# A hybrid decoder step: opening projections on unscaled rows, and the last expert outputs summed onto the residual in PSUM

## The reference, cut to what matters

```python
h = x * rsqrt(mean(x*x) + EPS) * norm1_g            # per row scale, per column gain
z = h @ w_in                                        # u (S5), xr, gate (RG-LRU), q, k, v, o, i/f gates (mLSTM)
# u goes through a diagonal complex SSM whose step sizes and angles come from
# exp(log_step), lambda_re, lambda_im; xr through a convolution and RG-LRU; q,k,v through chunked mLSTM
x1 = x + concat(s5, rglru, mlstm) @ w_out
g2 = rmsnorm(x1) * norm2_g
top4 = top_k(g2 @ router, 4); gates = softmax(top4)
for e in range(32):                                 # each token takes part in 4 experts
    y += gate[e] * (swiglu(g2 @ w1[e] + b1[e]) @ w2[e] + b2[e])
out = rmsnorm(x1 + y) * final_norm_g
```

## Time and profile before

| | us |
|---|---|
| time, median of 3 runs | 1101.66 (1099.63 to 1101.93) |
| the profiled execution, its own time | 1100.9 |
| its span | 1099.1 |
| TensorE busy | 1033.2 (94%) |
| VectorE, ScalarE, GpSimd busy | 317.2, 198.4, 95.4 |
| moved by DMA | 429.45 MB, mean 391 GB/s |

### The profile page before, as it was taken

The page is one execution under the profiler, slowest core; times in us unless marked ns, Lnnn a source line. Parts: engine busy times, 40 slices in busy tenths (PEclk is TensorE's granted clock), DMA queues, the critical chain, the costliest instruction groups (busy, mean ns, idle before and its releaser), DMA issues.

```text
span 1099.1 us, 13174 instructions
## 1 busy us (share of the span) xinstructions
PE 1033.2 (94%) x5132; PEld 434.6 (40%) x5132; DVE 317.2 (29%) x643; ACT 198.4 (18%) x418; POOL 95.4 (9%) x177
## 2 busy tenths in 40 slices
PE   8999999999999998999899988999899989998986
PEld 5767745334333433343333323332334233433322
DVE  6889456312131212120212112121212121202123
ACT  6543525301110201011000201020102010100002
POOL 6899000000000000000000000000000000000000
PEclk9999999999999999999999999999999999999999
DMA  7533799999999999999999999999999999999995
...
DMA packets 62052, 429.45 MB, mean 391 GB/s; under 512 B 12022, under 2 KB 25054, under 8 KB 33342
## 3 DMA queue, kind: packets, MB, share of 16 engines
...
## 4 chain that ended last, share of the span: by engine, by line
PE 53%; DMA 38%; DVE 5%; ACT 2%; issue 1%; SPq 1%; ACTq 0%; DVEq 0%
DMA ring_a<-in_exp_w_dram 32%; PE psum L2369 17%; PE psum L2404 12%; PE psum L2390 6%; DMA ring_b<-in_exp_w_dram 6%; PE psum L2303 3%; PE psum L2326 3%; PE psum L2134 3%; PE psum L1862 2%; PE psum L2413 1%; PE psum L2253 1%; PE psum L2259 1%; DVE rgb L1336 1%; SPq L444 1%; PE psum L2419 0%
## 5 line engine op out<-in xcount | busy, mean ns | idle before, releaser
L2369 PE MATMUL psum<-ring_a,xg 128*64 128x512 f32 x1200 | 341.8, 600 | 14.8 <-DMA ring_a<-in_exp_w_dram 14.8
L2404 PE MATMUL psum<-ring_a,aT 128*64 128x512 f32 x768 | 217.7, 596 | 9.9 <-DMA ring_a<-in_exp_w_dram 9.6
L2369 PEld LDWEIGHTS psum<-ring_a,xg 128*64 128x64 f32 x1200 | 102.8, 137 | 170.8 <-issue 165.4
L2369 PE MATMUL psum<-ring_b,xg 128*64 128x512 f32 x368 | 152.3, 598 | 7.7 <-DMA ring_a<-in_exp_w_dram 7.7
L1667 DVE TENSOR_TENSOR x<-x,psum 128x512 f32<-128x512 f32 x64 | 44.0, 687 | 384.1 <-PE psum L2326 384.1
L2390 PE MATMUL psum<-ring_a,xg 128*64 128x512 f32 x336 | 103.5, 609 | 14.5 <-DMA ring_b<-in_exp_w_dram 14.5
L2404 PEld LDWEIGHTS psum<-ring_a,aT 128*64 128x64 f32 x768 | 68.2, 137 | 111.8 <-issue 106.5
L2404 PE MATMUL psum<-ring_b,aT 128*64 128x512 f32 x256 | 104.1, 595 | 4.0 <-DMA ring_a<-in_exp_w_dram 2.5
L1736 DVE TENSOR_SCALAR acts<-psum 128x512 f32<-128x512 f32 x32 | 22.0, 687 | 224.4 <-PE psum L2390 208.0
L1040 ACT ACTIVATE acts<-acts 128x512 f32<-128x512 f32 x32 | 20.1, 627 | 297.5 <-DVE acts L1736 297.5
L2369 PEld LDWEIGHTS psum<-ring_b,xg 128*64 128x64 f32 x368 | 43.1, 136 | 75.5 <-issue 63.6
...
## 6 DMA issues: line engine op xcount, KB each, us to landing
...
```

The costliest lines, as they stand in the source:

```text
L2369: m = M(psum[64 * x:64 * x + 64, bk, :], xg[:, k, u, 64 * x:64 * x + 64], w[x][:, 512 * bk:512 * bk + 512], start=False, stop=(k == KD - 1))
L2404: m = M(psum[64 * x:64 * x + 64, 4 + nn, :], aT[:, 2 * j + s, 64 * x:64 * x + 64], w[x][:, 1024 * s + 512 * nn:1024 * s + 512 * nn + 512], ...
```

## The change

Five edits belong to the opening. The rows are turned as they arrive, without their scale: `turn_half` waits for the load alone, and all six halves go through VectorE, times `norm1_g`, into `raw_hT`, which lies where `q` and `k` come later. `u0` and `u1` are computed from `raw_hT`. The row scales become a row: TensorE spreads the three columns of `nst` over all partitions by products with the identity (bank `rstd`), in the middle of `u0`; ScalarE copies that to `rstd_row`; VectorE multiplies `raw_hT` by it into `hT` in two halves (`scaled`) and multiplies `u0` and `u1` by it on their way out of PSUM (`u_scaled`). The parameter rows are split: the 24 that are needed first (`norm1_g` and the lambdas) are in bank `vec`, the rest in `vec2`, turned within `u0`. ScalarE's exponential of the log steps comes first of all, one root is taken for all three tiles, and 14 warming products of TensorE become 9. SyncE issues the left half of the first weights before five of the parameter rows, and five loads of old states move from SyncE's queue to ScalarE's; TensorE turns those states after `xr0`, not before the gate products.

At the end, TensorE opens six result banks with a product whose columns are all zero while it waits for the last weights, VectorE copies the residual into them (`end_residuals`), and the six last combine products are added on top (`combine_end`). ScalarE and VectorE then read the sums in PSUM (`summed`), and the adding of VectorE goes.

```diff
-for _name, _n in (("norm1_g", 8), ("s5_d", 2), ("s5_glu_b", 2), ("rg_conv_w", 8), ("rg_conv_b", 2), ("rg_ba", 2),
-                  ("rg_bx", 2), ("rg_lambda", 2), ("ml_norm_g", 4), ("s5_lambda_re", 8), ("s5_lambda_im", 8)):
+for _name, _n in (("norm1_g", 8), ("s5_lambda_re", 8), ("s5_lambda_im", 8), ("s5_d", 2), ("s5_glu_b", 2), ("rg_conv_w", 8),
...
+NFIRST = 24
...
+_place(["vec", "vec2"], (6,))
+_place(["rstd"], (7,))
...
+        raw_hT = qkT[:].rearrange("p (k t) -> p k t", k=KD)
+        rstd_row = uT_rolled[:, 1, :]
...
+        def summed(i):
+
+            b = (6, 0, 2)[i]
+            return psum[0:TILES[i][1], b:b + 2, :].rearrange("p b n -> p (b n)")
...
-        END_UNITS = [(0, 0), (0, 1), (1, 0), (1, 1), (2, None)]
-        ADDED = (2, 4, 8)
+        END_UNITS = [(0, 0), (0, 1), (1, 0), (1, 1), (2, 0), (2, 1)]
+        END_BANKS = (6, 7, 0, 1, 2, 3)
...
+            for name, src in LAMBDAS:
+                load_vector(sp, name, src)
+            sp.dma_start(slot_view(0, 512)[:, :, 0:256], w_in_cols(WCH[0][0], 256)).then_inc(sem("w_in0"), 16)
...
-            A(nst[:, 12:13], nst[:, 8:9], ACT.Sqrt).then_inc(says_now("table_loaded"), 1)
+            act.wait_ge(sem("step_loaded"), 16)
+            A(step2[:], step2[:], ACT.Exp).then_inc(sem("step_exp"), 1)
             for i, (t0, n) in enumerate(TILES):
                 act.wait_ge(sem(f"x_loaded{i}"), 16)
                 A(x1[0:n, i, :], xn[0:n, i, :], ACT.Square, accum_out=nst[0:n, i:i + 1]).then_inc(says_now("ms_ready"), 1)
-                act.wait_ge(*at("ms_ready", i + 1))
-                A(nst[:, 4 + i:5 + i], nst[:, i:i + 1], ACT.Sqrt, scale=1.0 / D, bias=nst[:, 8:9]).then_inc(says_now("root_ready"), 1)
-            await_fill(act, "vec")
-            A(vecs[:, 0:NVEC + J5], bank("vec")[:, 0:NVEC + J5], ACT.Copy).then_inc(drained[FILLS["vec"][0]], 1)
-            act.wait_ge(drained[FILLS["vec"][0]], 1)
-            for i in range(2):
-                name = f"hT{2 * i + 1}"
-                await_fill(act, name)
-                for c in range(4):
-                    m = A(hT[:, 4 + c, 128 * i:128 * i + 128], bank(name)[:, 128 * c:128 * c + 128], ACT.Copy, scale=vec("norm1_g", 4 + c))
-                m.then_inc(drained[FILLS[name][0]], 1)
+            act.wait_ge(*at("ms_ready", 3))
+            A(nst[:, 4:7], nst[:, 0:3], ACT.Sqrt, scale=1.0 / D, bias=nst[:, 8:9]).then_inc(says_now("root_ready"), 1)
...
+            await_fill(act, "vec2")
+            A(vecs[:, NFIRST:NVEC], bank("vec2")[:, NFIRST:NVEC], ACT.Copy).then_inc(drained[FILLS["vec2"][0]], 1)
+            act.wait_ge(drained[FILLS["vec2"][0]], 2)
...
+            copy_out("rstd", rstd_row, bank("rstd")[:, 0:T])
...
-                await_fill(act, f"u{x}")
+                act.wait_ge(sem("u_scaled"), x + 1)
                 for half_ in range(2):
-                    A(uT_rolled[64 * half_:64 * half_ + 64, x, :], bank(f"u{x}")[64 - 64 * half_:128 - 64 * half_, 0:T], ACT.Copy).then_inc(
+                    A(uT_rolled[64 * half_:64 * half_ + 64, x, :], uT[64 - 64 * half_:128 - 64 * half_, x, :], ACT.Copy).then_inc(
                         sem("u_rolled"), 1)
-                act.wait_ge(sem("u_rolled"), 2 * x + 2)
-                copy_out(f"u{x}", uT[:, x, :], bank(f"u{x}")[:, 0:T])
 
             u_out(0)
+            u_out(1)
...
-                    A(psum[0:rows_, 4:6, :].rearrange("p b n -> p (b n)"), x1[0:rows_, i, :], ACT.Square,
+                    A(psum[0:rows_, 4:6, :].rearrange("p b n -> p (b n)"), summed(i), ACT.Square,
...
-            for i, (t0, n) in enumerate(TILES):
-                dve.wait_ge(*at("root_ready", i + 1))
-                dv(V.reciprocal(nst[:, 4 + i:5 + i], nst[:, 4 + i:5 + i]))
-                says(TSC(xn[0:n, i, :], xn[0:n, i, :], nst[0:n, 4 + i:5 + i], None, ALU.mult), "xn_ready", i + 1)
...
+            await_fill(dve, "vec")
+            dv(V.tensor_copy(vecs[:, 0:NFIRST], bank("vec")[:, 0:NFIRST]))
+            drains(V.tensor_copy(sm[:, 1, :], bank("vec")[:, NFIRST:NFIRST + J5]), "vec")
+            for k in (0, 1, 2, 4, 3, 5):
                 i, hf = k // 2, k % 2
                 t0, n = TILES[i]
...
-                drains(TT(hT[:, 4 * hf:4 * hf + 4, t0:t0 + n], bank(f"hT{k}").rearrange("p (k n) -> p k n", k=4)[:, :, 0:n],
+                drains(TT(raw_hT[:, 4 * hf:4 * hf + 4, t0:t0 + n], bank(f"hT{k}").rearrange("p (k n) -> p k n", k=4)[:, :, 0:n],
...
+            dve.wait_ge(*at("root_ready", 1))
+            V.reciprocal(nst[:, 4:7], nst[:, 4:7]).then_inc(sem("rstd_ready"), 1)
+
+            def scaled(hf):
+
+                k = slice(4 * hf, 4 * hf + 4)
+                TT(hT[:, k, :], raw_hT[:, k, :], spread(rstd_row.unsqueeze(1), 1, 4), ALU.mult).then_inc(sem("hT_scaled"), 1)
+
+            def u_scaled(x):
+
+                await_fill(dve, f"u{x}")
+                TT(uT[:, x, :], bank(f"u{x}")[:, 0:T], rstd_row, ALU.mult).then_inc(sem("u_scaled"), 1)
+                dve.wait_ge(sem("u_scaled"), x + 1)
+                dve.sem_inc(drained[FILLS[f"u{x}"][0]], 1)
+
+            dve.wait_ge(drained[FILLS["rstd"][0]], 1)
+            scaled(0)
+            u_scaled(0)
+            scaled(1)
...
+            u_scaled(1)
...
+            def end_residuals(gp, r):
+
+                dve.wait_ge(sem("combine_added"), gp * ADDS)
+                dve.wait_ge(sem("sgt_copied"), gp + 1)
+                dve.wait_ge(sem("aT_copied"), gp * 2 + 2)
+                dve.wait_ge(sem("end_opened"), r * len(END_UNITS) + len(END_UNITS))
+                for c, (i, nn) in enumerate(END_UNITS):
+                    n = TILES[i][1]
+                    V.tensor_copy(psum[0:n, END_BANKS[c], :], x1[0:n, i, 512 * nn:512 * nn + 512]).then_inc(sem("residual_in"), 1)
...
-                add_combined(t0 * 2 + (NPAIR - 1), END_BANKS, END_UNITS)
-                dve.wait_ge(sem("combine_added"), (t0 * 2 + NPAIR) * ADDS)
-                V.tensor_copy(st2[0:1, 13:14], x1[0:1, 0, 0:1]).then_inc(sem("swept"), 1)
+                end_residuals(t0 * 2 + (NPAIR - 1), r)
...
-                    STT(out=y_out[0:rows_, i, :], in0=x1[0:rows_, i, :], scalar=st2[0:rows_, 4 + i:5 + i], in1=gfb[0:rows_, :],
+                    STT(out=y_out[0:rows_, i, :], in0=summed(i), scalar=st2[0:rows_, 4 + i:5 + i], in1=gfb[0:rows_, :],
...
-            keep_warm(14)
+            keep_warm(9)
...
+            def scale_spread(k):
+
                 if k == 3:
-                    keep_warm(1)
-            keep_warm(2)
-            for k in range(6):
-                b, f = FILLS[f"hT{k}"]
-                pe.wait_ge(drained[b], f + 1)
-
-            def channels(name, c, col, between=None):
+                    rows_turned(1)
+                if k == 4:
+                    pe.wait_ge(sem("vec_loaded"), 16 * 8)
+                    await_bank(pe, "vec2")
+                    ends_fill(TR(bank("vec2")[:, 0:NVEC], vrow[0:NVEC, :], ident[0:NVEC, 0:NVEC]), "vec2")
+                if k == 5:
+                    pe.wait_ge(sem("rstd_ready"), 1)
+                    for i, (t0, n) in enumerate(TILES):
+                        m = M(bank("rstd")[:, t0:t0 + n], spread(nst[0:n, 4 + i:5 + i], 1, 128), ident[0:n, 0:n], start=True, stop=True)
+                    ends_fill(m, "rstd")
...
+            channels("u0", 0, 0, scale_spread, raw_hT)
+            channels("u1", 0, 128, None, raw_hT)
+            pe.wait_ge(sem("wgate_loaded"), 16)
+            pe.wait_ge(sem("hT_scaled"), 2)
+            gate_products()
...
+            def open_end(c):
+
+                n = TILES[END_UNITS[c][0]][1]
+                M(psum[0:n, END_BANKS[c], :], ident_bf[0:64, 0:n], spread(ident_bf[0:64, 127:128], 1, 512), start=True, stop=False).then_inc(
+                    sem("end_opened"), 1)
+
+            def combine_end(c):
+
+                i, nn = END_UNITS[c]
+                t0, n = TILES[i]
+                M(psum[0:n, END_BANKS[c], :], sgt[:, t0:t0 + n], yb[:, nn, :], start=False, stop=True).then_inc(sem("end_ready"), 1)
...
+                if last:
+                    pe.wait_ge(sem("sgt_copied"), gp + 1)
+                    for c in range(len(END_UNITS)):
+                        open_end(c)
...
+                for c in range(len(END_UNITS)):
                     pe.wait_ge(sem("y_copied"), gp * 2 + (1 if c == 0 else 2))
-                    combine(c, (6, 7, 0, 1, 2)[c], END_UNITS)
-
-            sweep(0, opening=True)
+                    pe.wait_ge(sem("residual_in"), r * len(END_UNITS) + c + 1)
+                    combine_end(c)
+                pe.sem_inc(sem("combine_ready"), len(UNITS))
```

107 lines of the change are left out of this document (57 added, 50 removed).

## The result

The changed kernel takes **1109.61 us** (median of 4 executions, 1108.48 to 1109.75), the kernel before in the same comparison 1100.78 (1099.63 to 1101.93): ratio 1.0079, 95% interval 1.0066 to 1.0092, so slower by 8.8 us. I had forecast 1100.4 us and at most 1103.0.

A forecast was written before the change was run, and what follows sets the result against it. VectorE's chain in the opening was taken to bound the kernel, through TensorE and the weight stream. Base 1101.3, plus 0.9 for the opening, minus 1.75 for the end, gave 1100.4 us, range 1098.0 to 1103.0.

The forecast's parts named there:

- The bound: Opening: VectorE's chain up to the S5 matrices holds TensorE at 128 us, and with it the weight stream and end.
- TensorE's wait for the scans: S5 scans, sign in the profile after: TensorE's longest wait for VectorE's scans grows from 1.4 to some 3.5 us.
- The end: After the last weights: squaring straight from PSUM ends the last scaling earlier; -1.75 us, bounds -2.0 and +0.4.
- six copies: End: VectorE's copies into PSUM take 4.1 us and finish 2.5 us ahead of the combine; doubled, they would cost 1.6.
- if that moves by d, I expect the end to move by d: Opening to end: a shift of the S5 matrices' start from 20.86 us passes on one for one, unless TensorE is later.
- d: Shift of the S5 matrices' start from 20.86 us: +1.2 before contention, +0.9 with it, bounds -0.9 and +4.2.
- -0.3 us, bounds -1.5 and +1.0: Second convolution: effect of VectorE and GpSimd shifting by 2 us against each other, taken as near zero.
- The few tenths: Opening: GpSimd's copies from 17.0 us on hold the two scaled operations, a few tenths left inside the sum's range.
- stages (b) and (c): Theory after measuring: (b) TensorE's long wait lowers its clock; (c) GpSimd catches up, starting together with VectorE's product E (lockstep).
- the rival that named this: Opening: lambda rows land late, deciding from bank vec full at 7.8; 1102.5 us, 1104 with worst contention; chance 0.15.
- The hand-over: Opening: passing the scales through TensorE and ScalarE to VectorE costs 1.8 us, with ScalarE's copy at 14.8.
- TensorE's lead behind `u1`: Opening: u1 ends on TensorE at 19.1 rather than 20.9, 1.8 us ahead.

The follow-up runs named there:

- e12: Kernel before with six more small VectorE operations ahead of the S5 matrices; 1107.9 us.
- e2: Kernel before with 22 more small VectorE operations ahead of the S5 matrices; 6.6 us slower than before.
- e3: Kernel before with 22 more small VectorE operations ahead of the S5 matrices and eight more small copies ahead of GpSimd's table; 11.8 us slower than before.
- e14: Kernel before with four more small copies ahead of GpSimd's table, VectorE's chain untouched; 1102.2 us.
- e13: Kernel before with six more small VectorE operations ahead of the S5 matrices and four more small copies ahead of GpSimd's table; 1102.1 us.
- e9: Changed kernel with 96 empty products of 128 columns in TensorE's wait for the scans; 1103.7 us.
- e4: Changed kernel with GpSimd's turning of states 4 to 7 also waiting for VectorE's product E of head j - 4; 1106.4 us.
- e6: Changed kernel with 48 empty products of 128 columns in TensorE's wait for the scans; 1107.6 us.
- e5: Changed kernel with TensorE's products for k3 moved ahead of those for S5 states 2 and 3; five times between 1103.4 and 1109.8 us.

## Why the prediction was wrong

**Right.** The bound: VectorE's chain sets the opening, and through TensorE the `w_out` load and the end. TensorE's wait for the scans grew (forecast "some 3.5 us", it was 5.75), though I saw no harm in it. The end: last scaling 15.51 us behind the last full step (forecast 15.5); six copies in 3.65 us (forecast 4.1), done 3.2 us before the combine at 1096.32 needs the banks.

**Wrong: "if that moves by d, I expect the end to move by d".** This is the step that failed most. My one-for-one doesn't hold on a chain that meets another engine on its way. With d = 0.9 (e12, by the profile) the end moved 6.8 us. I had the lock in the earlier trace rows and priced it as -0.3 us, bounds -1.5 and +1.0; it measured +2.8 in the changed kernel. I priced the stretch of the convolution alone, and took the positions of before as typical. They were favourable ones: in every profiled execution where VectorE and GpSimd were shifted against each other by a delay or by the changed opening, the way to the first scan was 2.2 to 3.1 us longer (column "scans" less column "S5 matr.", each against before; 2.2 in e2, 3.1 in e3; of e14's 2.3 a part is TensorE's), and none gained; with both moved (e13) it was 0.2 shorter. The few tenths that GpSimd was to cost the two `scaled` operations didn't come: both took 1.36 us, and where GpSimd's copy of 8 columns fell beside the second, it was the copy that took long (1.30 us instead of 0.20). And I did not ask what a longer wait does to TensorE's clock, nor to GpSimd, which in the kernel before started 0.6 to 1.4 us behind the scans that release it. Those two terms, which the sum has at nothing, are stages (b) and (c).

**Wrong: d itself.** Forecast +1.2 before contention, measured +4.4 in the profiled execution. Terms: `vec` copied at 8.44 instead of 6.9, as TensorE waited for the lambda row (+1.5; the rival that named this had that mechanism, "at 7.8 it decides", and a chance of 0.15, too low, but its price, 1102.5 to 1104 us, was one for one as well). The halves (3.52 us for six), the eleven small operations and the scalings (1.36, 0.45, 1.36) were sized right. The hand-over was not: the copy of the scales came at 17.85 for a forecast of 14.8, since TensorE's clock had fallen (0.50 at 11.5 to 13.5 us), so that `vec2` was full only at 15.9 and the table load came behind it. Before it fell TensorE had waited 2.01 and 1.25 us. In e9's profiled execution the waits were 0.53 and 1.26, the clock 1.00, ten of `u0`'s products took 2.66 us instead of 4.14, and the same opening had its S5 matrices at 22.89, within a microsecond of my 22.1. It is not the late lambda row that decides: in e4 TensorE had no such wait, `vec` was copied at 7.85 as in e6, and still the clock fell behind the second wait (1.28 us; 1.24 in e6, where it held) and the matrices came at 24.72 (23.18 in e6). Why it falls in one and holds in the other is open. With it went TensorE's lead behind `u1`, which I had at 1.8 us: the gate products start at 22.30 us, 1.3 later than before (21.02), and at 20.28 in e9.
```profile
10.00:11.50 1.50, 0.28 (x1) 0.00 (x0) 1.40 (x4) 0.71 (x2) 1.10 (x6) 0.87 1.14 342
11.50:13.50 2.00, 1.97 (x4) 1.51 (x5) 1.79 (x8) 0.00 (x0) 1.51 (x8) 0.50 0.80 139
```
```profile
9.00:10.60 1.60, 0.40 (x3) 0.10 (x1) 1.50 (x4) 0.94 (x2) 1.19 (x8) 1.00 1.09 388
10.60:12.60 2.00, 1.94 (x8) 1.60 (x9) 1.79 (x8) 0.00 (x0) 1.45 (x9) 1.00 0.96 215
```
(after, then e9). So d of this opening varies from +2.0 to +5.5: +2.0 and +2.3 where the clock held in `u0` (e9, e6), +3.9 to +5.5 where it fell (e4, after, e5). A right d would not have saved the forecast: e12, with d = 0.9 and less the end's 1.7, would be at some 1106 us (an estimate from the two runs), above my 1103.0.

**The account**, after against before. d gives 4.4; longer operations and waits up to the first scan 2.8 (7.20 - 4.39); state 2 a further 0.6 (waits of 1.68 and 1.10); the way to state 4 0.8 (94.32 - 85.76 = 8.56 in all); four products `E` 4.0. The fourth ends 12.45 us later (119.07 and 106.62). TensorE's numerators need it, and stood 1.76 us behind it before:
```profile
117.30 1.77 DVE L1462 TENSOR_TENSOR ring_a<-ring_a 128x384 f32<-128x384 f32 x1 [0.17 <-DVE ring_a L1455]
...
119.33 1.13 PE L2094 MATMUL psum<-ring_a 128*128 128x129 f32 x8 [1.38 <-DVE ring_a L1462]
```
```profile
105.83 0.79 DVE L1439 TENSOR_TENSOR ring_a<-ring_a 128x384 f32<-128x384 f32 x1 [0.17 <-DVE ring_a L1432]
...
108.38 1.16 PE L2036 MATMUL psum<-ring_a 128*128 128x129 f32 x8
```
(after, then before). The account is from one profiled execution of each kernel. 10.95 us arrive at the numerators, 10.93 at the `w_out` load and 10.48 at the last full step; less the end's 1.68 that is 8.8, the difference of the two spans (1107.9 and 1099.1).

**Open.** How much of the spread in e5 (1103.4 to 1109.8), e13 (1101.3 to 1106.5) and e14 (1100.4 to 1106.2) is the same switch of clock and lockstep. The kernel before itself took 1108.2 and 1108.8 us in two of its 19 executions beside e13 and e14, and 1099.4 to 1101.5 in the others. I have profiles of one execution each, so that is not shown, nor is what makes TensorE's clock fall in one opening and not in another.
